# A two-layer hybrid decoder step on one core: the low half of every fourth weight slab is formed by an adding DMA instead of a VectorE subtraction

## The chip, the cores and the metric

The kernel runs on one core of one Trainium2 chip. The metric is the time of the whole program on the device in microseconds (us), lower is better. The engines of the core are TensorE (PE, matmuls), VectorE (DVE), ScalarE (ACT), GpSimd (POOL) and SyncE (SP, which only issues DMAs here); ACT and POOL can issue DMAs too. All DMAs run on the core's 16 DMA engines.

## The reference

264 rows of activations (256 prompt positions and 8 samples) pass through two layers. What matters here is the one wide projection of a layer and what hangs on it:

```
z = h @ w_in                      # 2048 -> 7168, h is RMS-normalised
q, k, v, g_r, a, b, g_c = split(z)
u = a * sigmoid(b); c = causal depthwise conv of u, width 31
o = retention of rope(q), rope(k), v per head (8 heads of 128), with state
m = [groupnorm(o) * silu(g_r), (silu(layernorm(c)) @ w_pw2 + b) * silu(g_c)] @ w_out
h = x + rmsnorm(m); x = h + sigmoid(h @ w_gate) * rmsnorm(p @ w_ple)
```

All of it is float32, and the output has to have float32's accuracy.

## The kernel before

**Slabs.** Every product is made in tiles of 128 output features by 264 rows, summed over 2048 inputs. The weights of one tile are a slab of 128 partitions by 2048 numbers, 1 MB. PE multiplies in a rounded format (fp32r), so a weight w is split into a rounded high half and the rest: w = `whi` + `wlo`, and the activations likewise. `gemm` makes three matmuls per 128 inputs (high by high, high by low, low by high), 48 for a tile.

**The supply of a slab.** SP loads it into one of two places of `raw` (L379). ACT rounds it into `whi` (`next_hi`, L665), DVE subtracts, `wlo` = `raw` - `whi` (`lo`, L994). `whi` and `wlo` have four places each (slot = slab number modulo 4). So slab n's rounding waits for its load and for tile n-4 (semaphores `raw_even_in`, `raw_odd_in`, `tile_done`), its subtraction for the rounding (`hi_ready`), its tile for the subtraction (`lo_ready`), and the load of slab n+2 for the subtraction of slab n, because it takes the same place of `raw`.

**Stages of a layer.** Bodies of four tiles, all written out by hand in each engine's program order: 4 conv bodies (`conv_in` on ACT, `conv_b`, `conv_a`, `conv_u` and `taps` on DVE), 8 heads (`head` on PE, ACT and DVE: tiles q, k, v and gate of a head), 2 bodies of the conv group's gate (T_G), then the pointwise projection, the output projection, the per-layer embedding and its gate. In a head's body PE also does the retention of the head before it: after tile 0 `ret_turn` (L520, which transposes the normalised output `og` that ACT wrote, L771 and L773) and `ret_scores`, after tile 1 `ret_values`, after tile 2 `ret_samples` (L512, on the state `s_new` that DVE updated). ACT's order at the end of a head's body is: rounding of slab 2, rounding of slab 3, issue of the next state's load (L759), then `ret_normalise` (`og`), and the copies of tile 0 (`zs`, L721) once PE has it. DVE's order there is: subtraction of slab 2, `gz`, subtraction of slab 3, then `rt` (L1141). The 31 taps of the depthwise convolution are spread over DVE's program between these (L1060 to L1073). POOL takes the inverse square roots (`root`, `ret_root`). At the end of the conv stage ACT copies the samples into `ust` (L678) and issues three DMAs (L823, L824: convolution state out; L829: `p_in` in).

Of the kernel before, what the change touches and what calls it, by code (L numbers as in the profile page):

```python
# [35 lines left out]
P = 128  # L36
# [68 lines left out]
    return t + (TILES * l + 1)  # L105


BANKS = 4


# [14 lines left out]
class Signals:  # L125


    def __init__(self, nc):
# [14 lines left out]
        self.hi_ready = nc.alloc_semaphore("hi_ready")  # L143
        self.lo_ready = nc.alloc_semaphore("lo_ready")
        self.tile_done = nc.alloc_semaphore("tile_done")

        self.xhi_ready = nc.alloc_semaphore("xhi_ready")
        self.xin_ready = nc.alloc_semaphore("xin_ready")
# [75 lines left out]
def build(nc, ctx, x_t, p_t, s_ret, s_conv, vecs_d, consts_d, w_in, w_pw, w_out, w_ple, w_gate,  # L224
# [84 lines left out]
    def sm(name, at, n):  # L309
        return small[:, at:at + n]  # L310
# [7 lines left out]
    mv = small[:, 116:122].rearrange("p (c s) -> p c s", s=2)  # L318
    var_t, sc_t, nb_t, minus_mean = (small[:, 124 + 4 * i:127 + 4 * i] for i in range(4))
    minus_half = sm("minus_half", 140, 3)  # L320
    held = sm("held", 156, 1)

    accum_all = nc.alloc_psum_tensor("accum_all", [P, BANKS, 512], F32)
# [100 lines left out]

    @block.tensor
    def _(pe):
        def gemm(l, quad, bank, slab, j, at, k_tiles, operands, k_wait=None, among={}, fresh=True, weights=None):

            slot = (SLABS * l + j) % RING
            w_hi, w_lo = weights or (whi[:, slot, :], wlo[:, slot, :])  # L430

            pe.wait_ge(acc_free[bank], bank_free_at(l, quad))
            if fresh:

                pe.wait_ge(s.lo_ready, slab + (SLABS * l + 1))
            for k in range(k_tiles):
                if k_wait:  # L440
                    k_wait(k)
                if k in among:
                    among[k]()
                w = at + P * k
                hi, lo = operands(k)
                pe.matmul(accum[bank][:, 0:R], w_hi[:, w:w + P], hi, start=k == 0, stop=False)  # L446
                pe.matmul(accum[bank][:, 0:R], w_hi[:, w:w + P], lo, start=False, stop=False)  # L447
                mm = pe.matmul(accum[bank][:, 0:R], w_lo[:, w:w + P], hi, start=False, stop=k == k_tiles - 1)  # L448
            mm.then_inc(s.tile_done, 1)
# [95 lines left out]
        def head(l, h, prev, turn):  # L545

            for j in range(4):
                gemm(l, h + T_H // BANKS, j, 4 * h + (S_H + j), j, 0, KT, in_a)
                if turn and j == 0:
                    ret_turn(l, h - 2)  # L550
                if prev and j < 3:
                    (ret_scores, ret_values, ret_samples)[j](l, h - 1)
# [9 lines left out]
        for l in range(DEPTH):  # L562
# [6 lines left out]
                     among={1: {4 if l else 13: sum_x}, 2: {2 if l else 8: lambda: stat_bcast(l, ST_X)}}.get(j, {}))  # L569
            with pe.Fori(1, 4) as i:  # L570
                for j in range(4):
                    gemm(l, i, j, 4 * i + (S_C + j), j, 0, KT, in_a)

            pe.wait_ge(s.consts_in, 16)
            head(l, 0, False, False)
# [21 lines left out]
                     3: {2: lambda: ret_samples(l, 7), 8: variance_sum},  # L597
                     4: {9: lambda: stat_bcast(l, ST_LN), 14: lambda: ret_turn(l, 7)}}
            for t in range(CT):
                gemm(l, (T_G + t) // BANKS, t % BANKS, S_G + t, t % 4, 0, KT, in_a, among=among.get(t, {}))  # L600
                if t == 0:
                    ret_turn(l, 6)
                    ret_scores(l, 7)
# [55 lines left out]
    def _(act):  # L659
        def next_hi(l, body, j, tile):  # L660
# [3 lines left out]
            act.wait_ge(s.tile_done, tile_done_at(l, tile))  # L664
            nc.scalar.activation(whi[:, slot, :], raw[:, side, :], ACT.Copy).then_inc(s.hi_ready, 1)  # L665

        def conv_in(l, i):
            for j in range(4):
                ct = 2 * i + j // 2
                if j % 2 == 0:  # L670
                    next_hi(l, i, j, 4 * i + j)
                    act.wait_ge(acc_free[j], read_out_at(l, i))
                    nc.scalar.activation(tmp[2][:, :], tmp[0][:, :], ACT.Tanh, scale=0.5).then_inc(s.tanh_ready, 1)
                else:
                    next_hi(l, i, j, 4 * i + j)
                    act.wait_ge(s.u_ready, ct + (CT * l + 1))
                    ust_flat = ust[:, :, :, :].rearrange("p c k b -> p (c k b)")
                    nc.scalar.activation(ust_flat[:, bass.ds(ct * (TAPS * DEC) + PAD * DEC, DEC)],  # L678
                                         u_flat[:, bass.ds(ct * UW + PAD + SEQ,
                                                           DEC)], ACT.Copy).then_inc(s.ust_ready, 1)  # L680
# [32 lines left out]
        def head(l, h, prev, turn):  # L713
            n = h + HEADS * l
            if turn:
                ret_normalise(l, h - 1)

            act.wait_ge(s.tile_done, tile_done_at(l, 4 * h + T_H))
            if prev or l:
                act.wait_ge(s.rope_done, n)  # L720
            nc.scalar.activation(zs[:, 0, :], accum[0][:, 0:R], ACT.Copy)  # L721
            nc.scalar.activation(zw[0:64, 0, :], accum[0][64:P, 0:R], ACT.Copy)
            nc.scalar.activation(zw[64:P, 0, :], accum[0][0:64, 0:R], ACT.Copy).then_inc(acc_free[0], 1)
            if prev:
                ret_rows(l, h)
            next_hi(l, 4 + h, 0, 4 * h + T_H)

            act.wait_ge(s.tile_done, tile_done_at(l, 4 * h + (T_H + 1)))
            nc.scalar.activation(zs[:, 1, :], accum[1][:, 0:R], ACT.Copy)
            nc.scalar.activation(zw[0:64, 1, :], accum[1][64:P, 0:R], ACT.Copy)  # L730
            nc.scalar.activation(zw[64:P, 1, :], accum[1][0:64, 0:R], ACT.Copy).then_inc(acc_free[1], 1)
            if prev:
                ret_prompt_state(l, h)
            if turn:
                ret_round(l, h - 1)
            if prev:
                gate_silu(l, h)
            next_hi(l, 4 + h, 1, 4 * h + (T_H + 1))

            act.wait_ge(s.tile_done, tile_done_at(l, 4 * h + (T_H + 2)))  # L740
            nc.scalar.activation(vt[:, :], accum[2][:, 0:R], ACT.Copy).then_inc(acc_free[2], 1)
            if prev:
                ret_samples_out(l, h)
            act.wait_ge(s.kv_ready, n + 1)
            nc.scalar.activation(stack_cols[:, 0, 0:2, :], wide(ks[:, :], [P, 2, DEC]), ACT.Copy)
            nc.scalar.activation(stack_cols[:, 1, 0:4:2, :], wide(vs[:, :], [P, 2, DEC]),
                                 ACT.Copy).then_inc(s.stack_hi_ready, 1)
            next_hi(l, 4 + h, 2, 4 * h + (T_H + 2))

            next_hi(l, 4 + h, 3, 4 * h + (T_H + 3))  # L750
            if prev:
                state_in(l, h)

# [232 lines left out]
    def _(dve):  # L986
# [3 lines left out]
        def lo(l, body, j):  # L990
# [3 lines left out]
            v.tensor_tensor(wlo[:, slot, :], raw[:, side, :], whi[:, slot, :].bitcast(F32),  # L994
                            ALU.subtract).then_inc(s.lo_ready, 1)

        def x_lo(l, t):

            dve.wait_ge(s.xhi_ready, t + (KT * l + 1))
            v.scalar_tensor_tensor(rows(a_lo, t), rows(x, t), vec(l, t + V_PRE), rows(a_hi, t).bitcast(F32),  # L1000
                                   ALU.mult, ALU.subtract).then_inc(s.xin_ready, 1)
# [147 lines left out]
        def head(l, h, prev, turn, beside):  # L1149
# [44 lines left out]
            dve.wait_ge(s.tile_done, tile_done_at(l, 4 * h + (T_H + 3)))  # L1194
            dve.wait_ge(s.sg_ready, n + 1)
            v.tensor_tensor(gz[:, :], accum[3][:, 0:R], r_x[:, :], ALU.mult).then_inc(acc_free[3], 1)
            lo(l, body, 3)

        def parts(l, segments):

# [44 lines left out]
        for l in range(DEPTH):  # L1245
# [15 lines left out]
            taps(l, 0, 0, 0, CONV_0, 0, CONV_0 // 2)  # L1261
            lo(l, 1, 2)
            conv_a(l, 0, 3)
            lo(l, 1, 3)
            conv_u(l, 0, 3)
            taps(l, 0, 0, 0, CONV_0, CONV_0 // 2, CONV_0)
            seen = CONV_C + 1
            with dve.Fori(1, 4) as i:
                beside = parts(l, [((i - 1) * seen + (CONV_0 + 1), i, 0, CONV_C)])
                for j in range(4):  # L1270
                    (conv_b, conv_a)[j % 2](l, i, j)
                    beside[j]()
                    lo(l, 1 + i, j)
                    if j % 2:
                        conv_u(l, i, j)

# [178 lines left out]
    def _(pool):  # L1455
# [27 lines left out]
        def root(l, k):  # L1483

            pool.wait_ge(s.stat_scaled, stat_at(l, k))
            nc.gpsimd.tensor_tensor(rs, st, minus_half, ALU.pow).then_inc(s.stat_rs, 1)

        def ret_root(l, h):
# [4 lines left out]
            pool.wait_ge(s.pool_step, n + 1)  # L1493
            nc.gpsimd.tensor_tensor(nb_t, minus_mean, sc_t, ALU.mult).then_inc(s.ret_rs, 1)

        for l in range(DEPTH):
            root(l, ST_X)
            pool.wait_ge(s.sconv_step, 5 * (l + 1))
            nc.gpsimd.memset(vbd[:, :, :].bitcast(F32), 0.0)
            nc.gpsimd.memset(stack[:, :].bitcast(F32), 0.0)  # L1500
            nc.gpsimd.memset(og[:, 2, :], 0.0).then_inc(s.zeros_set, 1)
            with pool.Fori(0, HEADS - 1) as h:
                ret_root(l, h)
            root(l, ST_LN)
            ret_root(l, HEADS - 1)
            pool.wait_ge(s.mean_done, l + 1)
            pool.wait_ge(s.sum_done, stat_at(l, ST_LN))
            for n in range(OUT_FIRST):
                add_out(l, n)
            for pair in range(4):  # L1510
                add_ple(l, pair)
            add_out(l, OUT_FIRST)
            root(l, ST_M)
            for pair in range(4, PLE_HALF):
                add_ple(l, pair)
            root(l, ST_E)
            if l < DEPTH - 1:
                for n in range(KT):
                    add_x(l, n)
# [63 lines left out]
```

## Time and profile before

| | us |
|---|---|
| median of 3 runs | 1226.51 (1225.47 to 1227.88) |
| the profiled execution's own time | 1227.37 |
| its span, first to last instruction | 1225.4 |
| PE busy | 1197.9 (98%) |
| DVE busy | 926.9 (76%) |
| ACT busy | 604.7 (49%) |
| POOL busy | 94.3 (8%) |
| DMA read and written | 183 GB/s over the span |
| granted TensorE clock, mean | 0.995 |

Busy times count the instructions of an engine, not its waits. Matmuls are pipelined, so a busy PE says that it was fed, not more. The span and the program's own time are 2 us apart.

### The profile page before, as it was taken

Reading aid. Unit: us, or ns where it says so; the run is one execution under the profiler, and the core shown is the slowest. Engines: PE = TensorE matmul, PEld = TensorE weight load, DVE = VectorE, ACT = ScalarE, POOL = GpSimd, SP = SyncE. Lnnn points to the kernel's source line nnn. Section 1 sums busy time; section 2 is a strip of 40 time slices with the busy share of each in tenths; the row PEclk is TensorE's granted clock in tenths of the full one; section 3 lists DMA queues with packets and bytes.
Section 4 is the critical chain, followed back from the end, with each engine's and each line's share of the span. In section 5 each row is a group of like instructions: output and inputs, shape, how many; then the busy total and the mean of one; then the engine's idle time right before and its main releaser. Section 6 shows DMA issues by size and latency. Waiting matters only on the chain.

```text
span 1225.4 us, 25325 instructions
## 1 busy us (share of the span) xinstructions
PE 1197.9 (98%) x9822; PEld 1192.0 (97%) x9822; DVE 926.9 (76%) x1441; ACT 604.7 (49%) x908; POOL 94.3 (8%) x112
## 2 busy tenths in 40 slices
PE   5999999999999999999999999999999999999998
PEld 5999999999999999999999999999999999999998
DVE  6888899989986644487869879999899764436763
ACT  6433465555556444544544434555555454455351
POOL 0000000000000011311120000000000000123000
PEclk9999999999999999999999999999999999999999
DMA  7655655555545654415565565545555446442362
GB/s 264 212 202 177 207 197 191 192 189 178 205 147 200 224 190 172 170 43 201 190 221 196 195 200 179 207 176 192 192 202 191 157 172 239 173 172 103 136 226 87
DMA packets 42017, 225.69 MB, mean 184 GB/s; under 512 B 6112, under 2 KB 12256, under 8 KB 17888
## 3 DMA queue, kind: packets, MB, share of 16 engines
q1 hardware_dynamic: 27936, 199.37, 45.4%
q10 hardware_dynamic: 14016, 25.42, 6.4%
q8 instruction: 44, 0.72, 0.2%
q14 instruction: 21, 0.17, 0.0%
HBM read 210.97 MB, written 13.81 MB: 183 GB/s over the span
## 4 chain that ended last, share of the span: by engine, by line
PE 85%; DVE 7%; DMA 3%; ACT 2%; issue 2%; ACTq 1%; DVEq 0%; SPq 0%
PE accum_all L446 25%; PE accum_all L447 25%; PE accum_all L448 25%; DMA raw<-w_in 2%; PE ps L512 2%; DVE wlo L994 2%; ACT whi L665 1%; PE accum_all L537 1%; PE accum_all L538 1%; PE accum_all L539 1%; PE ps L462 1%; DMA raw<-w_gate 1%; DVE acc L1301 1%; ACTq L829 1%; DVE tmp L1070 0%
## 5 line engine op out<-in xcount | busy, mean ns | idle before, releaser
L446 PE MATMUL accum_all<-a_hi,whi 128*128 128x264 f32 x2080 | 596.6, 287 | 13.8 <-DVE wlo L994 13.8
L447 PE MATMUL accum_all<-a_lo,whi 128*128 128x264 f32 x2080 | 591.6, 284 | 0.0
L448 PE MATMUL accum_all<-a_hi,wlo 128*128 128x264 f32 x2080 | 591.3, 284 | 0.0
L994 DVE TENSOR_TENSOR wlo<-raw,whi 128x2048 fp32r<-128x2048 f32 x186 | 431.7, 2322 | 194.2 <-ACT whi L665 192.2
L665 ACT ACTIVATE whi<-raw 128x2048 fp32r<-128x2048 f32 x182 | 347.9, 1913 | 168.0 <-DMA raw<-w_in 65.1
L446 PEld LDWEIGHTS accum_all<-a_hi,whi 128*128 128x128 f32 x2080 | 394.2, 190 | 14.5 <-issue 13.8
L447 PEld LDWEIGHTS accum_all<-a_lo,whi 128*128 128x128 f32 x2080 | 394.4, 190 | 0.8
L448 PEld LDWEIGHTS accum_all<-a_hi,wlo 128*128 128x128 f32 x2080 | 392.4, 189 | 0.0
L446 PE MATMUL accum_all<-b_hi,whi 128*128 128x264 f32 x672 | 190.8, 284 | 0.0
L447 PE MATMUL accum_all<-b_lo,whi 128*128 128x264 f32 x672 | 190.4, 283 | 0.0
L448 PE MATMUL accum_all<-b_hi,wlo 128*128 128x264 f32 x672 | 190.3, 283 | 0.0
L447 PEld LDWEIGHTS accum_all<-b_lo,whi 128*128 128x128 f32 x672 | 126.6, 188 | 0.0
L446 PEld LDWEIGHTS accum_all<-b_hi,whi 128*128 128x128 f32 x672 | 126.6, 188 | 0.0
L448 PEld LDWEIGHTS accum_all<-b_hi,wlo 128*128 128x128 f32 x672 | 126.0, 187 | 0.0
L1070 DVE SCALAR_TENSOR_TENSOR c_buf<-u_buf,vecs,c_buf (+1 forms) x220 | 105.7, 481 | 0.4
L1070 DVE SCALAR_TENSOR_TENSOR tmp<-u_buf,vecs,tmp 128x256 f32<-128x256 f32 x204 | 98.0, 480 | 0.2
L891 ACT ACTIVATE sq<-accum_all 128x264 f32<-128x264 f32 x32 | 12.5, 391 | 88.1 <-PE accum_all L448 88.1
L1460 POOL TENSOR_TENSOR acc<-acc,sq 128x264 f32<-128x264 f32 x43 | 37.9, 881 | 200.1 <-ACT sq L891 138.2
L1492 POOL TENSOR_TENSOR small<-small 128x3 f32<-128x3 f32 x16 | 14.6, 913 | 371.9 <-DVE small L1133 371.9
L446 PE MATMUL accum_all<-c_hi,whi 128*128 128x264 f32 x128 | 36.3, 284 | 0.0
L447 PE MATMUL accum_all<-c_lo,whi 128*128 128x264 f32 x128 | 36.3, 283 | 0.0
L448 PE MATMUL accum_all<-c_hi,wlo 128*128 128x264 f32 x128 | 36.2, 283 | 0.0
(194 smaller groups left out, 1220.7 us busy)
## 6 DMA issues: line engine op xcount, KB each, us to landing
raw<-w_in SPq DMA_DIRECT2D x112, 1024.0 KB, 4.8
raw<-w_out SPq DMA_DIRECT2D x32, 1024.0 KB, 4.8
raw<-w_gate SPq DMA_DIRECT2D x32, 1024.0 KB, 4.8
s_new<-s_ret ACTq DMA_DIRECT2D x16, 512.0 KB, 3.6
ss_out<-s_new ACTq DMA_DIRECT2D x16, 512.0 KB, 2.6
raw<-w_pw SPq DMA_DIRECT2D x8, 1024.0 KB, 4.7
x<-x_t SPq DMA_DIRECT2D x4, 528.0 KB, 9.3
y_t<-x SPq DMA_DIRECT2D x4, 528.0 KB, 5.0
```

The source lines that it names most:

```text
L446: pe.matmul(accum[bank][:, 0:R], w_hi[:, w:w + P], hi, start=k == 0, stop=False)
L447: pe.matmul(accum[bank][:, 0:R], w_hi[:, w:w + P], lo, start=False, stop=False)
L448: mm = pe.matmul(accum[bank][:, 0:R], w_lo[:, w:w + P], hi, start=False, stop=k == k_tiles - 1)
L462: mm = pe.matmul(bank[:, c:c + 1], buf[:, r:r + P], ones[:, 0:1], start=n == 0, stop=n == len(bufs) - 1)
L512: mm = pe.matmul(ps_s1[0:QW, 0:P], q_diag[:, b, :], s_new[:, b * P:(b + 1) * P], start=b == 0, stop=b == DEC - 1)
L537: pe.matmul(out, whi[:, slot, w], hi, start=k == 0, stop=False)
L665: nc.scalar.activation(whi[:, slot, :], raw[:, side, :], ACT.Copy).then_inc(s.hi_ready, 1)
L891: nc.scalar.activation(sq[:, bank % 2, :], accum[bank][:, 0:R], ACT.Square).then_inc(s.msq_ready, 1)
L994: v.tensor_tensor(wlo[:, slot, :], raw[:, side, :], whi[:, slot, :].bitcast(F32), ALU.subtract).then_inc(s.lo_ready, 1)
L1070: v.scalar_tensor_tensor(out, src, w, out, ALU.mult, ALU.add).then_inc(s.tap_done, 1)
L1460: nc.gpsimd.tensor_tensor(buf, buf, square, ALU.add).then_inc(used, 1)
L1492: nc.gpsimd.tensor_tensor(sc_t, var_t, minus_half, ALU.pow).then_inc(s.pool_step, 1)
```

## The change

In 12 of the bodies' supplies per layer (conv bodies' and heads' slabs with j = 3, those that feed bodies 1 to 12, the last being tile 3 of the conv group's gate) the low half is made another way. ACT, after it has rounded slab 3 into `whi`, waits for that rounding's end and writes the negative of `whi` into `wlo` (`minus_hi`). POOL waits for this and issues a DMA that adds the same 1 MB of `w_in` from HBM into `wlo` (`sum_lo`), so that `wlo` becomes w - `whi`. PE's tile 3 waits for that DMA (`summed_lo_in`) besides `lo_ready`. DVE no longer subtracts for these slabs: it waits for the rounding and writes one element (`beat`), only to count `lo_ready` up in order, which also lets SP load into that place of `raw`. POOL's loop over the heads is written out.

```
+SUMMED = 12
@@ gemm (PE)
                 pe.wait_ge(s.lo_ready, slab + (SLABS * l + 1))
+            if summed is not None:
+                pe.wait_ge(s.summed_lo_in, 16 * summed + 16 * SUMMED * l)
@@ ACT
+        def minus_hi(l, body):
+            slot = (SLABS * l + 3) % RING
+            act.wait_ge(s.hi_ready, body * 4 + (SLABS * l + 8))
+            nc.scalar.activation(wlo[:, slot, :], whi[:, slot, :].bitcast(F32), ACT.Copy,
+                                 scale=-1.0).then_inc(s.minus_hi_ready, 1)
@@ conv_in (ACT)
                     next_hi(l, i, j, 4 * i + j)
+                    if j == 3:
+                        minus_hi(l, i)
@@ head (ACT)
             next_hi(l, 4 + h, 3, 4 * h + (T_H + 3))
+            minus_hi(l, 4 + h)
@@ DVE
+        def lo_summed(l, body):
+            dve.wait_ge(s.hi_ready, body * 4 + (SLABS * l + 4))
+            v.memset(beat, 0.0).then_inc(s.lo_ready, 1)
@@ head (DVE)
-            lo(l, body, 3)
+            lo_summed(l, body)
@@ POOL
+        def sum_lo(l, n, row):
+            slot = (SLABS * l + 3) % RING
+            pool.wait_ge(s.minus_hi_ready, n + SUMMED * l)
+            pool.dma_start(wlo[:, slot, :], w_in[bass.ds(row, P), :], accum_op=ALU.add).then_inc(s.summed_lo_in, 16)
...
             root(l, ST_X)
+            for i in range(1, 4):
+                sum_lo(l, i, P * (2 * i + in_row + 33))
+            sum_lo(l, 4, P * (in_row + 3 * HEADS))
...
+            sum_lo(l, 5, P * (in_row + 3 * HEADS + 1))
+            for h in range(HEADS - 2):
                 ret_root(l, h)
+                sum_lo(l, h + 6, P * (h + (in_row + 3 * HEADS + 2)))
+            ret_root(l, HEADS - 2)
+            sum_lo(l, 12, P * (in_row + 51))
```

ACT at the end of a head's body, before: the roundings of slabs 2 and 3, the state's load, and `og` for the next body.

```order
L665 ACTIVATE whi<-raw 128x2048 [waits tile_done,raw_even_in]
L664 REGISTER_ALU [waits raw_odd_in]
L665 ACTIVATE whi<-raw 128x2048 [waits tile_done]
L759 ISA [waits state_out,sample_out_done]
L759 DMA s_new<-s_ret 128x1024
L837 REGISTER_ALU
L837 COMPARE_AND_BRANCH
L771 ACTIVATE og<-ps,small 128x128 [waits ret_rs]
L771 ACTIVATE og<-ps,small 128x128
L773 ACTIVATE og<-ps,small 8x128
```

The same place of the changed kernel:

```order
L678 ACTIVATE whi<-raw 128x2048 [waits tile_done,raw_even_in]
L677 REGISTER_ALU [waits raw_odd_in]
L678 ACTIVATE whi<-raw 128x2048 [waits tile_done]
L683 ISA
L684 ACTIVATE wlo<-whi 128x2048 [waits hi_ready]
L782 ISA [waits state_out,sample_out_done]
L782 DMA s_new<-s_ret 128x1024
L860 REGISTER_ALU
L860 COMPARE_AND_BRANCH
L794 ACTIVATE og<-ps,small 128x128 [waits ret_rs]
L794 ACTIVATE og<-ps,small 128x128
L796 ACTIVATE og<-ps,small 8x128
```

A second pass over the slab now stands, with a wait for the first, ahead of the state's load and of `og`.

DVE at the same place, before (slab 2, the gate's tile, slab 3, then the next body's first steps):

```order
L994 TENSOR_TENSOR wlo<-raw,whi 128x2048 [waits hi_ready]
L1194 ISA
L1196 TENSOR_TENSOR gz<-accum_all,r_x 128x264 [waits sg_ready,tile_done]
L993 REGISTER_ALU
L994 TENSOR_TENSOR wlo<-raw,whi 128x2048 [waits hi_ready]
L1141 ISA [waits ret_ready,sg_ready,turn_done]
```

and in the changed kernel:

```order
L1017 TENSOR_TENSOR wlo<-raw,whi 128x2048 [waits hi_ready]
L1222 ISA
L1224 TENSOR_TENSOR gz<-accum_all,r_x 128x264 [waits sg_ready,tile_done]
L1022 REGISTER_ALU
L1023 MEMSET small 128x1 [waits hi_ready]
L1169 ISA [waits ret_ready,sg_ready,turn_done]
```

The second subtraction became a memset of one element with the same wait. POOL, from the first root of a layer on, now issues DMAs between its roots:

```order
L1517 TENSOR_TENSOR small<-small 128x3 [waits stat_scaled]
L1531 DMA wlo<-w_in 128x2048 [waits minus_hi_ready] x4
L1540 MEMSET vbd 128x1024 [waits sconv_step]
L1541 MEMSET stack 128x128
L1542 MEMSET og 128x128
L1531 DMA wlo<-w_in 128x2048 [waits minus_hi_ready]
L1523 TENSOR_TENSOR small<-small 128x3 [waits stat_ready]
L1525 TENSOR_TENSOR small<-small 128x3 [waits pool_step]
L1531 DMA wlo<-w_in 128x2048 [waits minus_hi_ready]
```

Before, no DMA stood in POOL's program; the roots and memsets are in the same order.

## Rows read from the trace of the kernel before

**Rows 1.** The page's first part: busy us (share of the span) and instructions.

```profile
span 1225.4 us, 25325 instructions
PE 1197.9 (98%) x9822; PEld 1192.0 (97%) x9822; DVE 926.9 (76%) x1441; ACT 604.7 (49%) x908; POOL 94.3 (8%) x112
```

**Rows 2.** PE's waits: instruction, what released it, us in total, times, longest.

```profile
PE accum_all L446 <- DVE wlo L994: 13.8, 1, 13.8
PE accum_all L537 <- DVE b_lo L1403: 3.6, 2, 1.8
PE ps L520 <- ACT og L773: 1.9, 2, 1.3
PE ps L512 <- DVE s_new L1116: 1.5, 2, 0.8
...
PE ps L496 <- DVE c_buf L1319: 0.5, 2, 0.3
...
PE ps L583 <- DVE pmat L1106: 0.5, 2, 0.3
```

**Rows 3.** The chain that ended last, 115 to 175 us: start, us, what.

```profile
121.07 0.22 ACT ust L678
...
122.70 3.68 ACTq L829
...
145.68 2.30 DVE wlo L994
148.14 4.71 DMA raw<-w_in
152.88 1.93 ACT whi L665
...
172.74 0.79 ACT og L771 x2
...
173.91 0.55 PE ps L520 x3
```

**Rows 4.** Stage table: busy us (instructions) by engine, PEclk, DMA share, GB/s.

```profile
92.00:115.00 23.00, 23.00 (x193) 23.00 (x192) 19.54 (x31) 8.72 (x8) 0.00 (x0) 1.00 0.52 182
119.40:132.70 13.30, 13.30 (x112) 13.30 (x112) 7.49 (x8) 6.05 (x9) 0.00 (x0) 1.00 0.78 184
...
230.50:258.70 28.20, 28.20 (x236) 28.04 (x234) 25.40 (x53) 15.56 (x31) 1.24 (x2) 1.00 0.55 194
```

**Rows 5.** The page's groups: busy us, mean ns | idle before, releaser.

```profile
L994 DVE TENSOR_TENSOR wlo<-raw,whi 128x2048 fp32r<-128x2048 f32 x186 | 431.7, 2322 | 194.2 <-ACT whi L665 192.2
L665 ACT ACTIVATE whi<-raw 128x2048 fp32r<-128x2048 f32 x182 | 347.9, 1913 | 168.0 <-DMA raw<-w_in 65.1
```

**Rows 6.** DVE in order of time, 226 to 238 us: start, us, instruction [idle before].

```profile
229.15 2.28 DVE L994 TENSOR_TENSOR wlo<-raw,whi 128x2048 fp32r<-128x2048 f32 x1
...
237.06 2.29 DVE L994 TENSOR_TENSOR wlo<-raw,whi 128x2048 fp32r<-128x2048 f32 x1 [1.82 <-ACT whi L665]
```

**Rows 7.** ACT in order of time, 220 to 230.6 us.

```profile
225.29 1.92 ACT L665 ACTIVATE whi<-raw 128x2048 fp32r<-128x2048 f32 x1 [2.52 <-DMA raw<-w_in]
225.50 0.37 ACTq L759 DMA_DIRECT2D s_new<-s_ret  x1
...
227.80 0.44 ACT L773 ACTIVATE og<-ps,small 8x128 f32<-8x128 f32 x1
230.56 0.39 ACT L721 ACTIVATE zs<-accum_all 128x264 f32<-128x264 f32 x1 [2.32 <-PE accum_all L448]
```

**Rows 8.** ACT's waits: us in total, times, longest.

```profile
ACT zs L721 <- PE accum_all L448: 22.6, 10, 2.9
```

**Rows 9.** DMA issues of the run: KB each, median us from issue to landing.

```profile
raw<-w_in SPq DMA_DIRECT2D x112, 1024.0 KB, 4.8
...
scs_out<-ust ACTq DMA_DIRECT2D x2, 960.0 KB, 10.3
```

**Rows 10.** The DMA view, 220 to 240 us: busy tenths of 16 engines in slices of 0.5 us.

```profile
DMA  0009197991000769800095989999899400000000
```

More of the change, by code:

```diff
@@ L145, in __init__ @@
         self.tile_done = nc.alloc_semaphore("tile_done")
+        self.minus_hi_ready = nc.alloc_semaphore("minus_hi_ready")
+        self.summed_lo_in = nc.alloc_semaphore("summed_lo_in")
         self.xhi_ready = nc.alloc_semaphore("xhi_ready")
@@ L320, in build @@
     minus_half = sm("minus_half", 140, 3)
+    beat = sm("beat", 164, 1)
     held = sm("held", 156, 1)
@@ L426, in _, with gemm @@
     def _(pe):
-        def gemm(l, quad, bank, slab, j, at, k_tiles, operands, k_wait=None, among={}, fresh=True, weights=None):
+        def gemm(l, quad, bank, slab, j, at, k_tiles, operands, k_wait=None, among={}, fresh=True, weights=None,
+                 summed=None):
             slot = (SLABS * l + j) % RING
@@ L547, in head @@
             for j in range(4):
-                gemm(l, h + T_H // BANKS, j, 4 * h + (S_H + j), j, 0, KT, in_a)
+                gemm(l, h + T_H // BANKS, j, 4 * h + (S_H + j), j, 0, KT, in_a,
+                     summed=h + 4 if j == 3 else None)
                 if turn and j == 0:
@@ L571, in _ @@
                 for j in range(4):
-                    gemm(l, i, j, 4 * i + (S_C + j), j, 0, KT, in_a)
+                    gemm(l, i, j, 4 * i + (S_C + j), j, 0, KT, in_a, summed=i if j == 3 else None)
             pe.wait_ge(s.consts_in, 16)
@@ L599, in _ @@
             for t in range(CT):
-                gemm(l, (T_G + t) // BANKS, t % BANKS, S_G + t, t % 4, 0, KT, in_a, among=among.get(t, {}))
+                gemm(l, (T_G + t) // BANKS, t % BANKS, S_G + t, t % 4, 0, KT, in_a, among=among.get(t, {}),
+                     summed=12 if t == 3 else None)
                 if t == 0:
@@ L1263, in _ @@
             conv_a(l, 0, 3)
-            lo(l, 1, 3)
+            lo_summed(l, 1)
             conv_u(l, 0, 3)
@@ L1272, in _ @@
                     beside[j]()
-                    lo(l, 1 + i, j)
+                    if j < 3:
+                        lo(l, 1 + i, j)
+                    else:
+                        lo_summed(l, 1 + i)
                     if j % 2:
@@ L1494, in ret_root @@
             nc.gpsimd.tensor_tensor(nb_t, minus_mean, sc_t, ALU.mult).then_inc(s.ret_rs, 1)
+        def sum_lo(l, n, row):
+            slot = (SLABS * l + 3) % RING
+            pool.wait_ge(s.minus_hi_ready, n + SUMMED * l)
+            pool.dma_start(wlo[:, slot, :], w_in[bass.ds(row, P), :], accum_op=ALU.add).then_inc(s.summed_lo_in, 16)
         for l in range(DEPTH):
+            in_row = 56 * l
             root(l, ST_X)
+            for i in range(1, 4):
+                sum_lo(l, i, P * (2 * i + in_row + 33))
+            sum_lo(l, 4, P * (in_row + 3 * HEADS))
             pool.wait_ge(s.sconv_step, 5 * (l + 1))
@@ L1501, in _ @@
             nc.gpsimd.memset(og[:, 2, :], 0.0).then_inc(s.zeros_set, 1)
-            with pool.Fori(0, HEADS - 1) as h:
+            sum_lo(l, 5, P * (in_row + 3 * HEADS + 1))
+            for h in range(HEADS - 2):
                 ret_root(l, h)
+                sum_lo(l, h + 6, P * (h + (in_row + 3 * HEADS + 2)))
+            ret_root(l, HEADS - 2)
+            sum_lo(l, 12, P * (in_row + 51))
             root(l, ST_LN)
```

## The prediction, made blind

> **What bounds the kernel now.** I read the page's first part first. TensorE (PE) is busy 1197.9 of 1225.4 us, VectorE (DVE) 926.9 and ScalarE (ACT) 604.7 [rows 1]. So work taken from DVE can only pay where PE waits for it. PE's waits say how much that is. 13.8 us is the first slab at the start and 3.6 us stands before the gate projection at the layers' ends; the change touches neither. In the conv, head and gate stages PE waits 1.9 us for `og`, 1.5 us for `s_new`, 0.5 us for `c_buf` and 0.5 us for `pmat` [rows 2]. The sum, 4.4 us, is all that a faster supply of slabs could give: 0.36%. Next, the chain of waits from 122 to 174 us shows why PE waits there at all: it leaves PE and runs through the queue of ACT's DMAs (3.68 us), ACT's rounding, DVE's subtraction and loads of `raw` that wait for that subtraction, until `og` lets PE go on at 173.9 us [rows 3]. Last, the stage table: a conv body takes 23.0 us with PE full (193 matmuls, so a tile of 48 takes 5.75 us), and a head body 28.2 us with DVE at 25.4 and ACT at 15.6 us [rows 4].
>
> **What it removes.** 24 subtractions (12 a layer) of 2.32 us by the page's mean [rows 5]: 55.7 us of DVE, and the one-element memset that takes their place lies, whatever it costs, in the idle time told of next. In a steady head body the last subtraction runs at 229.15, and DVE then waits 1.82 us before the next one at 237.06, for ACT's rounding, which is late because ACT first needs PE's scores [rows 6]. DVE that is 2.3 us earlier there waits 4.1 us instead of 1.8. So in steady bodies the relief is worth 0. It is worth something only in the chain of rows 3. There, at 145.7, the load for the next head is let go 2.3 us earlier, and at the end of the conv stage the copy of `ust` need not wait for DVE but only for ACT's own negative; I take 1.4 us for the second (the copy began at 121.1, and the negative ends near 119.5).
>
> **What it adds on ACT.** 24 passes of 128x2048. Their nearest row is the rounding itself, 1.91 us with the same shape [rows 5]; with the wait for the rounding's own end I take 2.0 to 2.1. Each stands between the rounding of slab 3 and the three operations on `og`, for which PE waits behind the next body's first tile. The price follows from the slack: at 225.29 the rounding starts, `og` is done at 228.24, and the next ACT operation, held by PE's tile, begins at 230.56 after 2.32 us idle [rows 7]. Over the run this wait comes 10 times, 22.6 us in total and at most 2.9: 2.26 in the mean [rows 8]. So 2.0 to 2.1 us fit in with 0.2 us to spare, and the negative by itself costs 0 in steady bodies. If nothing covered it, 12 to 14 head boundaries would cost 2 us each, 28 us. In the chain of rows 3 it is not covered: the rounding at 152.88 follows a load that now lands earlier, but ACT, which idled there, reaches it only 1.1 us earlier, since a negative stands ahead; and the one before `og` at 172.7 costs 2.0 in full. Balance per layer: 1.4 and 1.1 gained, 2.0 lost, so 0.5 gained, 1.0 us for both layers.
>
> **What it adds on the DMA engines.** 24 transfers of 1 MB from POOL's queue that add into `wlo`. No row of before shows one. The lower bound is a plain load of the same size, 4.8 us from issue to landing [rows 9], about 2.5 us of it on the engines: the two loads between 230.0 and 236.0 fill slices of 0.5 us by 97 tenths in all, 4.85 us [rows 10]. For the upper bound the farthest row is a DMA of 0.96 MB, 10.3 us under load [rows 9]; with twice its length, 20.6 us, the end stays open upward. Adding means that the old contents are read too, so I take twice the engine time, 5.0 us, about 7.5 us alone and 9 to 11 beside the loads. How long may it take? In a conv body PE comes back to tile 3 after three tiles, 17.2 us; less rounding and negative, 1.92 and 2.05, that leaves 13.3 us. In a head body tile 3 starts about 247.1 (the next boundary at 258.7 less two tiles of 5.8) and the negative ends near 229.3: 17.8 us. Both hold 9 to 11. The tightest is the sum for the first head: from 119.4 to 132.7 the engines are already 0.78 busy, 10.4 of 13.3 us [rows 4]; 5.0 more make 15.4, and it arrives in time only because it takes turns with transfers that nobody needs yet, those of the convolution state. There ACT's DMA queue, 3.68 us [rows 3], may take longer: I add 1 us a layer, 2.0 in all.
>
> **A page against the row.** The Trainium skill, Collectives: The Full Stack, "Part 3: Why 7× under link rate", has the add in a DMA engine cost no cycles of its own and halve the rate, since two sources are read. By it the sum is the one above; at the plain load's price no wait would be added at all and the forecast would be no change. The Trainium skill, DMA: Bandwidth & Descriptors, "Anatomy of one DMA", gives a transfer issued by GpSimd a fixed cost of about 2 us; no row here shows one. That would make the overlap below shorter.
>
> **What it moves.** The state load `s_new` stood behind the rounding and was issued at 225.50, while that ran [rows 7]; now it waits for the rounding's end, 1.9 us later, and its 1.3 us of engine time (half a load's) falls nearer to the next slab's load. The releases of two slabs of `raw` fall together near 229 instead of 2.3 us apart. The summing DMA begins there too. The engines are free now from 228.5 to 230.0 and then busy to 236 [rows 10]: first the load for tile 0's rounding, 2.5 us, landing near 233, wanted at 235.1, so with 2.1 us of slack. If the summing DMA shares the engines from 230.5 on with one turn in two by time, the load ends 2.1 us later, just in time; if its packets take two thirds, 4.2 later, 2.1 us too late; if it starts a microsecond later, 0. A late load delays rounding, subtraction, the load of slab 3 behind it, and `og`, where 0.2 us of slack is left. I take 0.7 us late less 0.3 slack, 0.4 us in each of the 5 steady bodies of a layer: 4.0 us. On POOL, behind a summing DMA that waits for ACT, stand only the roots for a head nearly a body later; 0.
>
> **Sum.** -1.0 + 2.0 + 4.0 = +5.0 us. The profiled execution took 1227.37 us (1225.4 of it span), the three timed ones have a median of 1226.51; 5 us on the median make **1231.5 us**, and 1232.4 for a profile's own time.
>
> **Rivals.**
> - *Hidden both ways* (0.27). The summing DMA starts late enough and takes as little as a plain one; the negative fits its 2.26 us. For it: both windows hold the estimate. Against: slack of 0.2 us. Gives 1224.5 to 1228.5, likeliest 1226.5.
> - *Loads crowded, small PE waits for `og`* (0.33, the forecast). From 0.2 to 1.5 us in 12 bodies: 1229 to 1244, likeliest 1231.5.
> - *The summing DMA is late for tile 3* (0.25). If adding is slower than two reads, say 16 us, the 8 conv windows (four a layer) miss by 2.7 us: 22 us, 1248. At 20 us they miss by 6.7 and the 16 head windows by 2.2: 54 and 35, 1315. It decides from 13.3 us on. Against it: only the assumed rate; nothing in the profile excludes it.
> - *Faster* (0.15). The chain of rows 3 is relieved and nothing takes its place: `s_new` 1.5 and `og` 1.9 us of waits go, less 0.4: 1223.5. It decides if the loads of heads 1 and 2 land within 5 us and the summing DMA stays off them.
>
> The measurement tells 0.2%, 2.5 us, from no change. Faster by more: 0.15. Within it: the hidden case 0.25 and the lower edge of the forecast, together 0.29. Slower: 0.56. The range from 1222.5 to 1270 leaves out the late case beyond about 18 us; the forecast's own is 1229 to 1244.
>
> **What would show it.** Right: the PE waits for `og` rise from 1.9 to some 6 us and more in number; DVE falls by 54 us and its wait for ACT's rounding grows; ACT rises by 46 us; PE's wait on the summing semaphore is 0; loads of `raw` land in 4.8 us in the median but in 6 to 9 in the heads' first slab. Wrong: PE idle before tile 3 of conv bodies (the DMA is slower than 13.3 us); no new PE wait at all (hidden); or `og` waited for at every boundary by the same length (the negative does not fit). The forecast fails most easily by the unknown rate of adding.

## The result, and the profile after

The changed kernel took 1276.24 us in the median of 6 runs (1266.64 to 1281.25), the kernel before 1226.96 us beside it (1225.47 to 1227.92). That is 49 us slower by the medians. The ratio, which goes by the means, is 1.0389, with a 95% interval from 1.0342 to 1.0436. The forecast was 5 us slower, with a range up to 1270.

The page of the profiled execution (1266.64 us, the fastest of the six) answers to [rows 1]: busy us, share and instructions.

```profile
span 1264.9 us, 25367 instructions
PE 1210.2 (96%) x9822; PEld 1200.6 (95%) x9822; DVE 876.3 (69%) x1441; ACT 649.1 (51%) x932; POOL 117.0 (9%) x136
```

DVE lost 50.6 us of work and ACT gained 44.3, against 54 and 46 forecast. PE, which has the same 9822 matmuls, is busy 12.3 us longer. PE's waits, which answer to [rows 2]:

```profile
PE accum_all L457 <- DVE wlo L1017: 14.1, 1, 14.1
PE ps L531 <- ACT og L796: 12.6, 9, 2.4
PE ps L523 <- DVE s_new L1144: 11.8, 4, 4.5
PE accum_all L457 <- DMA wlo<-w_in: 5.7, 2, 3.1
PE accum_all L548 <- DVE b_lo L1434: 3.6, 2, 1.8
```

The waits for `og` and `s_new` went from 3.4 to 24.4 us, and 5.7 us for the summing DMA are new: 26.7 us. With PE's 12.3 us that makes 39.0 of the 39.5 us by which the span grew. The 12.3 us fit the clock: TensorE's granted clock was 0.50 in nine stretches, 34.1 us in all, against two with 10.2 us before (the last microseconds of the program left out), and half of the 23.9 us more is 12. Seven of the nine lie at or within 1.5 us behind a wait of 1.8 to 4.5 us for `og` or `s_new`. The stage table shows a stretch of 3.3 us behind the wait for `s_new` in head 1 (columns as in [rows 4]):

```profile
158.00:163.50 5.50, 1.30 (x12) 1.09 (x11) 5.42 (x8) 4.08 (x8) 0.00 (x0) 1.00 0.90 292
164.00:167.30 3.30, 3.30 (x17) 3.30 (x16) 3.30 (x8) 0.78 (x2) 0.00 (x0) 0.50 0.62 241
167.50:173.00 5.50, 5.50 (x48) 5.50 (x47) 5.35 (x19) 2.13 (x3) 0.00 (x0) 1.00 0.51 188
```

PE got 12 matmuls into 5.5 us, then the granted clock was 0.50 (1.2 GHz) and 17 matmuls took 3.3 us, then 48 took 5.5 us again at 1.00 (2.4 GHz). The mean granted clock fell from 0.995 to 0.986.

The wait for `s_new` in head 1 ends a chain that can be followed in the trace (start, us, what; it answers to the load at 148.14 in [rows 3]):

```profile
148.64 7.47 DMA raw<-w_in
156.14 1.92 ACT whi L678
158.08 1.11 DVE wlo L1017
...
161.61 0.66 DVE s_new L1143
162.27 0.66 DVE s_new L1144
```

The load was issued 0.5 us later than before and took 7.47 us instead of 4.71, with a summing DMA issued at 148.24. Rounding, subtraction and `s_new` follow it, and PE waited 4.2 us there, where it had waited 0.7.

The DMA issues and queues of the changed kernel, which answer to [rows 9]:

```profile
q1 hardware_dynamic: 27936, 199.37, 44.3%
q0 software_dynamic: 3456, 25.17, 10.1%
...
raw<-w_in SPq DMA_DIRECT2D x112, 1024.0 KB, 5.6
...
wlo<-w_in POOLq DMA_DIRECT2D x24, 1024.0 KB, 13.3
```

A sum occupies the engines for 0.101 x 1264.9 / 24 = 5.3 us, against 5.0 us in the forecast, but lands 13.3 us after its issue. Its 3072 packets of 8 KB (the other 384 have 4 bytes) take 0.101 x 1264.9 x 16 / 3072 = 0.67 us each, those of the loads 0.443 x 1264.9 x 16 / 27936 = 0.32 us, with 4128 smaller packets counted in. From 302.5 to 308.0 us both queues were at work:

```profile
q0 software_dynamic: 95, 0.78, 68.6%
q1 hardware_dynamic: 91, 0.71, 32.1%
```

The packets went about one for one, and the sum had two thirds of the engines.

ACT in order of time at the boundary into the second body of the loop over heads, which answers to [rows 7]:

```profile
206.13 1.92 ACT L678 ACTIVATE whi<-raw 128x2048 fp32r<-128x2048 f32 x1 [2.51 <-DMA raw<-w_in]
208.08 1.91 ACT L684 ACTIVATE wlo<-whi 128x2048 fp32r<-128x2048 f32 x1
...
210.58 0.43 ACT L796 ACTIVATE og<-ps,small 8x128 f32<-8x128 f32 x1
210.92 0.36 ACT L743 ACTIVATE zs<-accum_all 128x264 f32<-128x264 f32 x1
```

The negative took 1.95 us and there is no idle time left ahead of `zs`: PE already waited for `og`.

### The profile page after: what moved, and what is told of

Read it like the earlier page. It is cut to its first block, busy times and chain, and to the rows that moved or that the text cites. A ratio compares the mean times of both kernels' runs of the same rounds, so it can differ in the third digit from the quotient of the medians.

```text
span 1264.9 us, 25367 instructions
## 1 busy us (share of the span) xinstructions
PE 1210.2 (96%) x9822; PEld 1200.6 (95%) x9822; DVE 876.3 (69%) x1441; ACT 649.1 (51%) x932; POOL 117.0 (9%) x136
## 3 DMA queue, kind: packets, MB, share of 16 engines
q1 hardware_dynamic: 27936, 199.37, 44.3%
q0 software_dynamic: 3456, 25.17, 10.1%
## 4 chain that ended last, share of the span: by engine, by line
PE 57%; DVE 17%; DMA 14%; ACT 6%; issue 5%; ACTq 2%; DVEq 0%; SPq 0%
PE accum_all L457 16%; PE accum_all L458 16%; PE accum_all L459 16%; DMA raw<-w_in 9%; DVE wlo L1017 7%; ACT whi L678 4%; DMA raw<-w_gate 3%; DMA wlo<-w_in 2%; DVE c_buf L1098 1%; DVE tmp L1098 1%; PE ps L523 1%; ACTq L852 1%; PE accum_all L548 1%; PE accum_all L549 1%; PE accum_all L550 1%
## 5 line engine op out<-in xcount | busy, mean ns | idle before, releaser
L457 PE MATMUL accum_all<-a_hi,whi 128*128 128x264 f32 x2080 | 598.3, 288 | 19.8 <-DVE wlo L1017 14.1
L1017 DVE TENSOR_TENSOR wlo<-raw,whi 128x2048 fp32r<-128x2048 f32 x162 | 376.2, 2323 | 236.1 <-ACT whi L678 234.2
L457 PEld LDWEIGHTS accum_all<-a_hi,whi 128*128 128x128 f32 x2080 | 395.3, 190 | 21.2 <-issue 14.1
L684 ACT ACTIVATE wlo<-whi 128x2048 fp32r<-128x2048 f32 x24 | 46.1, 1919 | 0.8
L523 PE MATMUL ps<-s_new,q_diag 128*72 128x128 f32 x256 | 33.4, 288 | 11.8 <-DVE s_new L1144 11.8
L1531 POOL DMA_DIRECT2D wlo<-w_in x24 | 22.0, 916 | 236.3 <-ACT wlo L684 236.3
## 6 DMA issues: line engine op xcount, KB each, us to landing
wlo<-w_in POOLq DMA_DIRECT2D x24, 1024.0 KB, 13.3
```

Source lines behind the costliest of these rows:

```text
L523: mm = pe.matmul(ps_s1[0:QW, 0:P], q_diag[:, b, :], s_new[:, b * P:(b + 1) * P], start=b == 0, stop=b == DEC - 1)
L684: nc.scalar.activation(wlo[:, slot, :], whi[:, slot, :].bitcast(F32), ACT.Copy, scale=-1.0).then_inc(s.minus_hi_ready, 1)
L1531: pool.dma_start(wlo[:, slot, :], w_in[bass.ds(row, P), :], accum_op=ALU.add).then_inc(s.summed_lo_in, 16)
```

## The experiments

Theory 1: the summing DMA shares the engines with the loads, a packet of each in turn, and so delays the loads that the next body's roundings wait for; `s_new` and `og` come late behind them. Theory 2: the extra pass on ACT delays `og`. Theory 3: any further megabyte costs, or tile 3 waits for the sum itself.

**e1_no_dma** takes the DMAs out:

```
-            pool.dma_start(wlo[:, slot, :], w_in[bass.ds(row, P), :], accum_op=ALU.add)...
-                pe.wait_ge(s.summed_lo_in, 16 * summed + 16 * SUMMED * l)
+                pe.wait_ge(s.minus_hi_ready, summed + SUMMED * l)
```

> Leaves out the summing DMAs: wlo of these 24 slabs holds only the negative, and PE waits for the negative instead. Theory 1 (the summing DMA's 628 ns packets take turns with the 324 ns packets of the raw loads, the next body's first slab comes late, and og and s_new behind it): without the DMA nearly all of the loss goes, 1225 to 1229 us, loads of raw back at 4.8 us in the median, PE's waits for og and s_new together under 5 us. Rival theory 2 (the 24 extra ACT passes delay og): the loss stays for the most part, 1250 to 1270 us, og waited for at most head boundaries.

Measured: 1231.19 us beside 1226.47, ratio 1.0051 (1.0034 to 1.0068). The DMAs make 45 of the 49 us. In the profile, taken of the fastest execution (1226.02 us), PE waits 4.6 us for `og`, 4 times; loads land in 4.9 us. The time is 2 us above what theory 1 expected: the negative by itself costs something.

**e2_no_negative** takes the negatives out; POOL waits for the rounding:

```
-            pool.wait_ge(s.minus_hi_ready, n + SUMMED * l)
+            pool.wait_ge(s.hi_ready, 4 * n + SLABS * l + 4)
```

> Leaves out the negatives: the DMA adds w_in onto whatever wlo held, and waits for the rounding instead. It starts 1.9 us earlier. Theory 1: most of the loss stays, 1245 to 1275 us, since the DMA shares the engines with the same loads; ACT's slack of 2 us returns and saves some of it. Theory 2: 1225 to 1230 us. A third theory, that tile 3 waits for the DMA itself, expects its 5.7 us of waits to go and the rest to stay.

Measured: 1282.54 us, ratio 1.0462 (1.0434 to 1.0491), slower than the changed kernel itself and outside all expectations. PE's waits:

```profile
PE ps L523 <- DVE s_new L1142: 31.5, 14, 7.6
...
PE ps L531 <- ACT og L794: 11.9, 14, 1.8
...
PE accum_all L457 <- DMA wlo<-w_in: 2.1, 1, 2.1
```

The sums land in 9.4 us instead of 13.3: with 1.9 us of a start they get ahead of the loads, and PE now waits for `s_new` 14 times. Most of the 3.9 us lies ahead of the transfer: in the heads the first packet comes 1.6 to 1.7 us after the issue, in the changed kernel 4.0 to 5.1 us after it in 14 of 16. Why it comes so late there is open. What matters is when the DMA meets the next body's loads. Theory 2 falls as the main cause.

**e3_plain_copy** has the same DMA without adding:

```
-            pool.dma_start(wlo[:, slot, :], w_in[bass.ds(row, P), :], accum_op=ALU.add)...
+            pool.dma_start(wlo[:, slot, :], w_in[bass.ds(row, P), :])...
```

> The same DMA from the same queue without adding: wlo becomes the weights, not the low half. Theory 1: packets of about 320 ns take turns one for one with the loads, 2.6 us of engine time instead of 5.3, loads slowed to a half and not to a third: lands in 7 to 9 us, 1230 to 1250 us. If it is the queue of POOL and not the adding that costs, the time is that of the changed kernel, 1266 to 1281 us.

Measured: 1262.0 us, ratio 1.0286 (1.0254 to 1.0317), above the range expected of theory 1 and below that of its rival. Its queue takes half of the engines' time, 5.4% against 10.1%, so adding doubles the work; but PE waits 21.3 us for `og` and 8.3 us for `s_new`, and 35 of the 49 us of loss stay. It lands in 9.5 us in the median, above the expected 7 to 9. A plain megabyte at this moment costs seven tenths of an added one. What the queue of POOL itself does was not tried by itself: the same copy from another queue was not run. I had made the share of the engines too important and the moment too little.

**e4_relief_only** has neither negatives nor DMAs, only DVE's relief.

> Leaves out negatives and DMAs and keeps only DVE's relief: wlo of these slabs keeps old numbers. It measures all that the relief can give. By PE's waits of before that is at most 4.4 us: 1222.5 to 1226.5 us, likeliest 1223.5, with no PE wait for og or s_new. If the relief were worthless, as in the steady bodies, 1226.5 to 1227.

Measured: 1222.83 us, ratio 0.9981 (0.9962 to 0.9999). PE's waits for `og` and `s_new` are 0.3 us each. So all that there was to gain is 3.6 us by the medians and 2.3 by the ratio, whose interval reaches from 0.1 to 4.7. By the medians e1 against e4, 8.4 us, is the negatives' price; by the two profiled executions it is 4.3 us (spans of 1224.2 and 1219.9), which is just what PE waits more for `og`, 4.6 less 0.3.

**e5_quarters** issues the sum in four pieces of 512 columns:

```
-                pe.wait_ge(s.summed_lo_in, 16 * summed + 16 * SUMMED * l)
+                pe.wait_ge(s.summed_lo_in, 64 * summed + 64 * SUMMED * l)
...
+            for c in range(4):
+                pool.dma_start(wlo[:, slot, 512 * c:512 * c + 512], w_in[bass.ds(row, P), 512 * c:512 * c + 512],
+                               accum_op=ALU.add).then_inc(s.summed_lo_in, 16)
```

> The summing DMA in four pieces of 512 columns, with rows of 2 KB instead of 8. Theory 1 with turns by the packet: the summing packets shrink to 160 to 200 ns against the loads' 324, the loads keep two thirds of the engines while both run, the first load of the next body is late by 1 us instead of 4: 1235 to 1255 us, the summing DMAs land later (14 to 18 us) and tile 3 of conv bodies may wait. Rival: the engines are shared by bytes, and the size of the packets changes nothing: 1270 to 1280 us.

Measured: 1324.01 us, ratio 1.080 (1.077 to 1.083), far above the expectation. Its queue and PE's waits:

```profile
q0 software_dynamic: 13824, 25.17, 11.8%
```

```profile
PE accum_all L457 <- DMA wlo<-w_in: 76.5, 16, 14.1
...
PE ps L531 <- ACT og L796: 0.7, 1, 0.7
```

A packet of 2 KB takes 0.118 x 1322.3 x 16 / 12288 = 0.20 us. On the shares theory 1 said it right. From 847.5 to 852.0 us both queues were at work:

```profile
q1 hardware_dynamic: 135, 0.97, 55.1%
q0 software_dynamic: 137, 0.26, 37.7%
```

The packets went one for one again, and this time the loads had the larger part. But that is not why the sum misses tile 3, 16 times by up to 14.1 us. POOL did not issue the four pieces together:

```profile
POOL wlo L1532 <- issue: 219.4, 31, 11.8
```

31 times POOL stood between two pieces, waiting for nothing that the profile shows, 219.4 us in total. The last piece of a sum was issued 6.7 to 18.5 us after the first, and the sum was complete 13.5 to 26.6 us after its first issue. What holds POOL there is open. Nor do the vanished waits for `og` and `s_new` (0.7 us and none) show that the loads were in time: their median is 5.9 us, against 5.6 in the changed kernel, and PE, held at tile 3 for 76.5 us, came later to everything behind it. The run shows how the packets share the engines; it does not show what the smaller share would cost by itself.

**e6_after_loads** lets the sums of the heads wait until the next body's two first loads have landed:

```
+            if n >= 5:
+                for g in (SLABS * l + 4 * n + 4, SLABS * l + 4 * n + 5):
+                    pool.wait_ge(raw_in[g % RAW], 16 * (g // RAW + 1))
```

> In the heads (sums 5 to 12 of a layer) POOL waits until both loads of the next body's first two slabs have landed before it issues the summing DMA. Theory 1: the loads that decide are undisturbed, s_new and og are waited for as in e1_no_dma: 1229 to 1238 us, with some waits for tile 3 at the end of heads if the DMA then lands more than 16.6 us behind the boundary. Rival theory 3 (any further megabyte on the engines costs, wherever it is put): 1255 to 1280 us.

Measured: 1253.8 us, ratio 1.0217 (1.0199 to 1.0236), between the two theories. The waits for `og` fall to 1.7 us and for `s_new` to 3.2 us, as theory 1 has it. In head 1 the load that took 7.47 us in the changed kernel takes 4.9 us here. Instead of those waits PE now waits 20.5 us for the sum, 8 times, 11.8 us of it in head 1 of the two layers (4.2 and 7.6). In the steady heads the sums are issued some 7 us behind the boundary and land 9.4 us later.

**e7_conv_only** keeps only the four sums of a layer made in conv bodies; the heads' slabs are subtracted by DVE.

> Only the four slabs made in the conv bodies are summed by DMA, those of the heads are subtracted by DVE as before: 8 sums instead of 24. If the loss comes from the heads' bodies as the trace says, 1229 to 1240 us; the part that stays is the wait for s_new in head 1 and the first conv body. If every sum costs the same, a third of the loss stays: 1243 us.

Measured: 1235.39 us, ratio 1.0060 (1.0042 to 1.0079). A third of the sums make a sixth of the loss. Of PE's waits 5.6 us are for the sum, in the first conv body of each layer (2.9 us at most). The expected wait for `s_new` in head 1 did not stay: `s_new` is waited for 1.5 us, as in the kernel before.

**e8_late_og_first** adds to e6 the order of ACT: `og` first, then the negative.

```
                 ret_normalise(l, h - 1)
+            if prev:
+                minus_hi(l, 3 + h)
...
             next_hi(l, 4 + h, 3, 4 * h + (T_H + 3))
-            minus_hi(l, 4 + h)
...
                     ret_normalise(l, 7)
+                    minus_hi(l, 11)
```

> e6_after_loads, and the heads' negatives moved behind the three operations on og, into the 2.3 us in which ACT waits for the next tile. Theory 1 with theory 2's small share (1 to 5 us, by e1_no_dma against e4_relief_only 8 us): og is not waited for at all, 1223 to 1228 us, at best the 1222.8 of e4_relief_only. If the summing DMA, now up to 2 us later, misses tile 3: waits of PE on it and 1230 to 1245 us.

Measured: 1245.2 us, ratio 1.0164 (1.0138 to 1.0190), at the upper end of what was expected if the sum misses tile 3. `og` is not waited for at all. ACT at a steady boundary, in order of time:

```profile
232.55 1.92 ACT L678 ACTIVATE whi<-raw 128x2048 fp32r<-128x2048 f32 x1 [2.74 <-DMA raw<-w_in]
...
235.05 0.44 ACT L797 ACTIVATE og<-ps,small 8x128 f32<-8x128 f32 x1
235.40 1.90 ACT L684 ACTIVATE wlo<-whi 128x2048 fp32r<-128x2048 f32 x1
237.66 0.39 ACT L745 ACTIVATE zs<-accum_all 128x264 f32<-128x264 f32 x1 [0.36 <-PE accum_all L459]
```

The negative lies in ACT's idle time, and 0.36 us of it is left. What remains is at four places, the first conv body and head 1 of each layer: 12.9 us of PE waits for the sum, 4 times, up to 4.6, and in head 1 also 3.2 us for `s_new`. In head 1 of the first layer the sum is late because it waits for the loads: POOL is through with its memsets at 146.8 us and issues it at 157.88, 11.05 us later, where the changed kernel issued it at 148.24.

**e10_heads_only** keeps of e8 only the sums 6 to 12 of a layer, 14 in all.

> The sums 6 to 12 of each layer alone (slabs made in heads 1 to 7), issued after the next body's two loads have landed and with the negative behind og, as in e8_late_og_first, which lost nothing in these bodies. Slabs made in the conv bodies and head 0 are subtracted by DVE. If relief is worth nothing where DVE waits for ACT anyway: 1226 to 1228 us, no change, PE waits for no summing DMA. If the relief in these bodies were worth something: under 1224. If 14 MB more on the engines cost in any place: over 1230.

Measured: 1232.67 us (1229.85 to 1234.62) beside 1225.72, ratio 1.0053 (1.0034 to 1.0072). The expectation of no change is missed by 5 us; over 1230 was expected if 14 MB more on the engines cost in any place, and that is what came. In the profile of 1229.85 us PE waits 2.9 us for the sum (twice), 3.4 for `og`, 1.2 for `s_new`. Even with the best place found, these sums gain nothing and cost a little.

**e9_swap** is the kernel before with one edit, to see where the 3.6 us of relief lie:

```
                     beside[j]()
-                    lo(l, 1 + i, j)
                     if j % 2:
                         conv_u(l, i, j)
+                    lo(l, 1 + i, j)
```

> The kernel before, with one edit: in the conv bodies 1 to 3 DVE runs conv_u ahead of the subtraction instead of behind it, so the copy of ust need not wait 2.3 us for a subtraction. No slab is summed by DMA. If the relief measured by e4_relief_only (3.6 us) came from the chain at the end of the conv stage: 1222.5 to 1225 us, PE's waits for s_new and og fall from 3.4 to under 1.5 us. If it came from the heads' own subtractions (the load released 2.3 us earlier behind head 0): 1225.5 to 1227 us and the waits stay.

Measured: 1220.53 us beside 1225.72, ratio 0.9951 (0.9934 to 0.9968): faster than both kernels and 2 us below the expected range. The waits for `og` and `s_new` are no longer among PE's. DVE and then ACT at the end of the conv stage, against 121.07 and 122.70 in [rows 3]:

```profile
116.53 0.43 DVE L1044 SCALAR_TENSOR_TENSOR u_buf<-tmp,tmp 128x264 f32 x1
116.87 2.28 DVE L994 TENSOR_TENSOR wlo<-raw,whi 128x2048 fp32r<-128x2048 f32 x1
```

```profile
117.18 0.21 ACT L678 ACTIVATE ust<-u_buf  x1 [1.51 <-DVE u_buf L1044]
...
118.80 1.23 ACTq L829 DMA_DIRECT2D p_in<-p_t  x1
```

The copy of `ust` comes 3.9 us earlier on the clock of the two spans, and the issue of `p_in` takes 1.23 us instead of 3.68. The chain of [rows 3] starts that much earlier. In e4_relief_only the copy began at 117.75 us, nearly as early, but there the issue of `p_in` took 5.04 us, so that ACT's next copy came at 124.90 us and in e9_swap at 120.41. Whether that makes e9's median lower than that of e4 is not settled; the kernel before itself ranged from 1222.5 to 1230.5 in these runs.

**e11_again** is the changed kernel once more, for a second profile.

> The changed kernel unchanged, for a second profile, since its timed runs spread from 1266 to 1281 us and the first profile is at the lower end. If the spread lies in when the summing DMA and the loads meet, the waits for og, s_new and the DMA differ between the two profiles by some 10 us and the granted clock moves with them; if it lies elsewhere, the waits are the same and PE's busy time differs.

Measured: 1277.42 us, a usual run and not the fastest. Its page and waits:

```profile
PE 1212.8 (95%) x9822; PEld 1202.8 (94%) x9822; DVE 876.8 (69%) x1441; ACT 648.3 (51%) x932; POOL 116.4 (9%) x136
```

```profile
PE ps L531 <- ACT og L796: 19.2, 10, 3.0
...
PE ps L523 <- DVE s_new L1144: 12.6, 6, 3.8
PE accum_all L457 <- DMA wlo<-w_in: 6.4, 2, 3.4
```

The three waits are 38.2 us against 30.1 in the first profile, and PE is busy 2.6 us more: 10.7 us, the difference of the spans (1275.6 to 1264.9). So these two executions differ by these waits and the clock, as expected if the spread of the changed kernel comes from how its DMAs meet; that itself is argued and not shown.

## Why the prediction was wrong

**What held.** PE waits bound the gain: 3.4 us of waits for `og` and `s_new` were seen, and the medians of e4 give 3.6 us. A sum costs twice a plain load's engine time: 5.3 us against 0.054 x 1261.6 / 24 = 2.8 in e3. The Trainium skill, Collectives: The Full Stack, "Part 3: Why 7× under link rate", says the same of an add; by that rule the trace agrees. The mechanism of the forecast, crowded loads and then waits for `og`, is the one that the runs show: without the DMAs 45 of the 49 us go (e1), and the chain of head 1 goes through a late load.

**Crowded loads: the mis-sized term.** This is the step that failed. It was "0.4 us in each of the 5 steady bodies of a layer: 4.0 us". Measured, the waits for `og` and `s_new` rose by 21.0 us in one profile and by 28.4 in the other; of the 21.0, 7.2 us are `s_new` in head 1 and 13.8 us lie in the bodies behind it, for which the 4.0 stood. Three things were wrong in it. First, the share: I gave the sum's packets two thirds as a bound, worked out 2.1 us late and took 0.7. The slack was read too long as well: the load given as landing near 233 landed at 233.83, 1.3 us before 235.1 and not 2.1. The packets' times, 0.67 and 0.32 us, say two thirds, the trace has 68.6% against 32.1% while both are at work, and with packets of 2 KB it was 37.7% against 55.1% (e5). The Trainium skill, DMA: Bandwidth & Descriptors, "Queues, rings and completion order", says that an engine goes round its queues by the packet; the runs agree, with 95 packets against 91 in one stretch and 137 against 135 in the other. Second, only the load for the first rounding was priced; the load behind it took 13.1 us at the boundary near 210 us, against 4.8 at the same place before. Third, head 1, where the chain of [rows 3] has no slack at all, was treated as a place of gain. Set matmul for matmul against the trace of before, PE loses 5.1 us there in layer 0, around 158 us (12 matmuls in 5.5 us, above), and 5.8 us in layer 1.

**The clock was left out.** No term stood for what PE pays after a wait. PE is busy 12.3 us longer, of the 39.5 in the span: 34.1 us at a granted clock of 0.50 (1.2 GHz) instead of 10.2. In the stretch of 3.3 us shown above 17 matmuls ran, where there is room for 29 at full clock.

**Tile 3's wait.** The windows, 13.3 and 17.8 us, were right for steady bodies: there the sums, at most 15.0 us from issue, were not waited for in the heads. In the first conv body the row was not read: ACT's rounding of slab 3 waited for its load and came late, so only 8.8 us were left from the issue of the sum to tile 3, and PE waited 3.1 and 2.6 us, 5.7 in all. The rival that had the sum late put it at 13.3 us for all eight conv windows; it happened in two.

**The relief's place.** "There, at 145.7, the load for the next head is let go 2.3 us earlier" was a wrong reading: the load at 148.14 waits for the subtraction at 145.68, which is slab 2's and stayed. The other place, the copy of `ust`, is enough for the relief: e9, which only reorders the conv bodies, takes away all the waits for `og` and `s_new`. In the changed kernel even this was taken back. The copy of `ust` began at 119.07 us, 2.0 us earlier than before (1.4 forecast), but the issue of `p_in` behind it took far longer:

```profile
120.86 6.41 ACTq L852 DMA_DIRECT2D p_in<-p_t  x1
```

That is 2.7 us more than the 3.68 of [rows 3], where 1 us a layer was put in, and ACT's next copy began at 127.32 us against 127.17.

**The negative.** "The negative by itself costs 0 in steady bodies" nearly holds in the profiled execution of e1: of its 4.6 us of waits for `og`, 3.9 are at 170.9 and 772.5 us, the place of each layer where the prediction had the negative cost 2.0 in full, and 0.7 in the bodies behind them. By the medians e1 against e4 has the negatives at 8.4 us; what the slower executions of e1 add to the 4.3 of the profiled ones was not profiled and is open.

**Step by step.** DVE fell by 50.6 us (54 forecast), ACT rose by 44.3 (46), the waits for `og` rose beyond the 6 us named (12.6), the loads of `w_in` land in 5.6 us in the median (4.8 said). Open is also how much of e3's 35 us is the transfer itself and how much its moment.

## What to carry to other kernels

When the tightest engine is 98% busy, list its waits first; here those that the change could touch were worth 3.6 us by the medians, and swapping two DVE operations took them without any new traffic. A DMA that is put beside the prefetches must be placed by when the next loads go out, and its packets' length against theirs sets what part of the engines each of them gets. Cutting a transfer into pieces changes that part, but here POOL then issued the pieces up to 11.8 us apart. Price each new wait of TensorE with the clock that follows it, not by its own length alone.

## What was not expected of the hardware

A sum, which is twice the work, and a plain one differed by 14 us in the end (1276 and 1262), while leaving the negatives out and so starting 1.9 us earlier made the sums land in 9.4 us and the kernel 6 us slower. The same 1 MB took 9.2 to 15.0 us from issue to landing within one execution, and its first packet came 1.6 us after the issue at the earliest and 5.1 at the latest. POOL stood 219.4 us between the pieces of its sums (e5) without a cause in the profile. A sum in four pieces costs more on the engines, 11.8% of 1322 us against 10.1% of 1265, 6.5 us each instead of 5.3.
